# Rotating both token tiles on VectorE, and turning the attention rows by SBUF block moves instead of TensorE transposes

## The reference, cut to what matters

```
h = rmsnorm(x, g_mix);  z = h @ w_in            # 1024 x 5888
aq, ak, av, rq, rk, rv, rg, ga, gb = split(z)   # 512,128,128,512,512,1024,1024,1024,1024
aq, ak = rope_half(aq), rope_half(ak)           # 8 query heads, 2 key heads, of 64
ya = sliding_window_sink_attention(aq, ak, av, sinks) @ w_a
rq, rk = retention_rotation(rq), retention_rotation(rk)   # 4 heads of 128, pairs of neighbours
yb = (normed retention(rq, rk, rv) * silu(rg)) @ w_b
x = x + (sigmoid(ga) * ya + sigmoid(gb) * yb) @ w_out
x = x + square(relu(rmsnorm(x, g_mlp) @ w_up)) @ w_down
```

## Time and profile before

| what | value |
|---|---|
| median of the runs | 1015.03 us |
| profiled execution | 1015.36 us |
| its span | 1013.4 us |
| TensorE matmul busy | 1005.9 us, 99% |
| VectorE busy | 719.7 us, 71% |
| ScalarE busy | 504.4 us, 50% |
| GpSimd busy | 170.3 us, 17% |

### The profile page before, as it was taken

How to read it: one execution, slowest core, us unless ns; L and a number is a source line. 1 busy time by engine, 2 the same in 40 slices (tenths; PEclk the granted TensorE clock), 3 DMA queues, 4 the chain that set the end, 5 groups by cost and what they waited for, 6 DMA issues and landing times.

```text
span 1013.4 us, 13611 instructions
## 1 busy us (share of the span) xinstructions
PE 1005.9 (99%) x5677; PEld 851.7 (84%) x5677; DVE 719.7 (71%) x817; ACT 504.4 (50%) x620; POOL 170.3 (17%) x129
## 2 busy tenths in 40 slices
PE   9999999999999999999999999999999999999997
PEld 7888888888888888888788888888887899899796
DVE  5887746766565565797756667888877757789974
ACT  6545544454444545445554454444468545654352
POOL 0520010000000000430010020000000139159730
PEclk9999999999999999999999999999999999999999
DMA  9794455555555555594544557656654754355451
GB/s 337 252 306 128 163 166 166 169 175 196 193 184 206 166 176 178 186 293 164 166 150 142 168 147 279 197 185 208 199 175 135 233 182 166 125 166 145 116 188 42
DMA packets 100765, 185.47 MB, mean 183 GB/s; under 512 B 8840, under 2 KB 16096, under 8 KB 100576
## 3 DMA queue, kind: packets, MB, share of 16 engines
q1 hardware_dynamic: 100528, 184.51, 55.3%
q10 hardware_dynamic: 176, 0.09, 0.0%
HBM read 179.12 MB, written 3.15 MB: 180 GB/s over the span
## 4 chain that ended last, share of the span: by engine, by line
PE 99%; DMA 0%; DVE 0%; ACT 0%; SPq 0%; issue 0%; DVEq 0%; ACTq 0%
PE bank L766 14%; PE bank L768 12%; PE bank L769 12%; PE bank L1082 11%; PE bank L791 9%; PE bank L795 8%; PE bank L802 8%; PE bank L1086 6%; PE bank L1164 2%; PE bank L1388 1%; PE bank L964 1%; PE bank L948 1%; PE bank L773 1%; PE bank L783 1%; PE bank L1375 1%; PE bank L793 1%
## 5 line engine op out<-in xcount | busy, mean ns | idle before, releaser
L1868 DVE TENSOR_TENSOR w_lo<-arena,w_hi 128x2048 fp32r<-128x2048 f32 (+1 forms) x80 | 185.2, 2324 | 103.6 <-ACT w_hi L1476 103.3
L1868 DVE TENSOR_TENSOR w_lo<-raw,w_hi 128x2048 fp32r<-128x2048 f32 (+1 forms) x78 | 181.2, 2331 | 87.4 <-ACT w_hi L1476 87.2
L1476 ACT ACTIVATE w_hi<-raw 128x2048 fp32r<-128x2048 f32 (+1 forms) x83 | 157.1, 1893 | 100.3 <-PE bank L769 70.8
L1476 ACT ACTIVATE w_hi<-arena 128x2048 fp32r<-128x2048 f32 (+1 forms) x80 | 151.3, 1891 | 104.2 <-PE bank L769 80.4
L1082 PE MATMUL bank<-hT,w_hi 128*128 128x512 f32 x504 | 123.4, 391 | 0.0
L766 PE MATMUL bank<-w_hi,hT 128*128 128x512 f32 (+1 forms) x296 | 114.1, 386 | 0.0
L1082 PEld LDWEIGHTS bank<-hT,w_hi 128*128 128x128 f32 x504 | 92.2, 188 | 17.6
L2470 POOL TENSOR_TENSOR rstd<-mean,const 128x1 f32<-128x1 f32 (+1 forms) x16 | 9.1, 579 | 557.8 <-DVE mean L1877 388.5
L769 PE MATMUL bank<-w_hi,hT 128*128 128x512 f32 (+1 forms) x256 | 97.9, 382 | 0.0
L768 PE MATMUL bank<-w_lo,hT 128*128 128x512 f32 (+1 forms) x256 | 97.9, 382 | 0.0
L791 PE MATMUL bank<-w_hi,hT 128*128 128x512 f32 (+1 forms) x216 | 83.8, 391 | 0.0
(11 more groups left out here) (347 smaller groups left out, 1891.0 us busy)
## 6 DMA issues: line engine op xcount, KB each, us to landing
arena<-in_w_in SPq DMA_DIRECT2D x22, 1024.0 KB, 5.2
raw<-in_w_in SPq DMA_DIRECT2D x20, 1024.0 KB, 5.7
arena<-in_w_up SPq DMA_DIRECT2D x16, 1024.0 KB, 5.8
raw<-in_w_up SPq DMA_DIRECT2D x16, 1024.0 KB, 5.3
arena<-in_w_down SPq DMA_DIRECT2D x16, 1024.0 KB, 5.2
raw<-in_w_down SPq DMA_DIRECT2D x16, 1024.0 KB, 5.2
raw<-in_e_w_in SPq DMA_DIRECT2D x6, 1024.0 KB, 5.2
arena<-in_e_w_in SPq DMA_DIRECT2D x6, 1024.0 KB, 5.2
```

The source lines that it names most:

```text
L1476: act.activation(w_hi[:, p % SPLIT_RING, :, 0:n], raw_at(p)[:, :, 0:n], copy).then_inc(hi_ready, 1)
L1868: dve.tensor_tensor(w_lo[:, s, :, 0:n], raw_at(p)[:, :, 0:n], w_hi[:, s, :, 0:n].bitcast(F32), ALU.subtract).then_inc(lo_ready, 1)
```

## The change

`A_SLOTS` is 6: four pairs of query heads and two key heads. `rotate_halves` no longer writes the rotated queries in place and the keys to `ak_twice`; it writes all to `a_rows`, ordered by block of 32 features and then slot. Per layer, sixteen transfers of 48 KB from SBUF to SBUF (32 partitions, two rows of 768 bytes in each) move block b of token block i to partitions 32b to 32b + 31, and VectorE turns the result into `aT`, which is `aqT` and `akT` in one. SP issues them behind the four fetches of the retention rows, and ahead of the load of piece 14. VectorE turns them behind the retention rows and ahead of the split of piece 13. The twelve transposes, their three copies and GpSimd's rotations are gone. TensorE waits for `aT_ready` between the retention scores and the first attention scores.

```diff
-        ak_twice = area(16896, T, KV_HEADS * 2 * HEAD)
+        aT = area(11776, PAIRS + KV_HEADS, SEQ)
+        a_moved = area(15360, T * BLOCKS, A_SLOTS * BLOCK)
+        a_rows = area(16896, T, BLOCKS * A_SLOTS * BLOCK)
@@ rotate_halves
-            twice = ak_twice[:, t, :].rearrange("p (v c e d) -> p v c e d", v=KV_HEADS, c=2, e=2)
+            to = a_rows[:, t, :].rearrange("p (c e s d) -> p s c e d", c=2, e=2, s=A_SLOTS)
+            aq, bq = (v[:, 0:Q_HEADS, :, :].rearrange("p (i c) e d -> p i c e d", c=2) for v in (a4, b4))
             for e, op in ((0, ALU.subtract), (1, ALU.add)):
-                o.mark(eng.tensor_tensor(z[:, 0:Q_HEADS, e, :], a4[:, 0:Q_HEADS, e, :], b4[:, 0:Q_HEADS, e, :], op))
+                o.mark(eng.tensor_tensor(to[:, 0:PAIRS, :, e, :], aq[:, :, :, e, :], bq[:, :, :, e, :], op))
                 for c in range(2):
-                    last = eng.tensor_tensor(twice[:, :, c, e, :], a4[:, Q_HEADS:, e, :], b4[:, Q_HEADS:, e, :], op)
+                    last = eng.tensor_tensor(to[:, PAIRS:, c, e, :], a4[:, Q_HEADS:, e, :], b4[:, Q_HEADS:, e, :], op)
@@ SP, behind the load of piece 13
+                    fetch_blocks(r_moved, r_bounce, r_blocks)
+                    for t in range(T):
+                        sp.wait_ge(rope_done[t], l + 1)
+                    rows_out = a_moved.rearrange("p (t i) x -> p t i x", t=T)
+                    width = A_SLOTS * BLOCK
+                    for i in range(BLOCKS):
+                        for b in range(BLOCKS):
+                            sp.dma_start(rows_out[b * BLOCK:(b + 1) * BLOCK, :, i, :],
+                                         a_rows[i * BLOCK:(i + 1) * BLOCK, :, b * width:(b + 1) * width]).then_inc(a_blocks, 16)
@@ TensorE, window
-                if g == 4:
-                    (waits for both rotations, twelve transposes)
                 if g == 5:
                     pe.wait_ge(rT_ready, l + 1)
-                    pe.wait_ge(akT_ready, l + 1)
...
-                    pe.wait_ge(aqT_first, l + 1)
-                    pe.wait_ge(aqT_second, l + 1)
+                    pe.wait_ge(aT_ready, l + 1)
@@ VectorE
+            def turn_blocks(dst, src, slots, across=False):
+                rows_in = src.rearrange("p u (f s) -> p u s f" if across else "p u (s f) -> p u s f", s=slots)
+                return dve.transpose(dst.rearrange("p s (u q) -> p u s q", q=BLOCK), rows_in)
...
-                    rotate_pairs(dve, order, l, 0, z_ga, between=lambda part: step(l * PIECES + 2 * AQ + 1 + part))
+                    rotate_pairs(dve, order, l, 0, z_ga)
+                    step(l * PIECES + 2 * AQ + 1)
+                    rotate_pairs(dve, order, l, 1, z_gb)
+                    step(l * PIECES + 2 * AQ + 2)
                 if g == 3:
-                    rotate_halves(dve, order, l, 0, z_ga)
+                    for t in range(T):
+                        rotate_halves(dve, order, l, t, (z_ga, z_gb)[t])
...
                     if g == 5:
                         dve.wait_ge(r_blocks, 16 * BLOCKS * (l + 1))
-                        dve.transpose(rT.rearrange(...), r_moved.rearrange(...)).then_inc(rT_ready, 1)
+                        turn_blocks(rT, r_moved, 2 * RET_HEADS).then_inc(rT_ready, 1)
+                        dve.wait_ge(a_blocks, 16 * BLOCKS * BLOCKS * (l + 1))
+                        turn_blocks(aT, a_moved, A_SLOTS).then_inc(aT_ready, 1)
@@ GpSimd
-                rotate_pairs(pool, order, l, 1, z_gb)
-                rotate_halves(pool, order, l, 1, z_gb)
```

More of the change, by code:

```diff
@@ L34 @@
 BLOCKS = P // BLOCK
+A_SLOTS = PAIRS + KV_HEADS
 ATT2_HEADS = 4
@@ L400, in build_program @@
         rT_ready = sem("rT_ready")
[L401 to L404, removed]
+        a_blocks = sem("a_blocks")
+        aT_ready = sem("aT_ready")
         tanh_ready = sem("tanh_ready")
@@ L663, in load, with fetch_blocks @@
                 n[0] += 1
+            def fetch_blocks(dst, src, done):
+                for b in range(BLOCKS):
+                    at = slice(b * BLOCK, (b + 1) * BLOCK)
+                    sp.dma_start(dst[at, :, :], src.rearrange("(u q) (b x) -> b q u x", q=BLOCK, b=BLOCKS)[b]).then_inc(done, 16)
             def blocks_moved(l, piece):
@@ L987, in window @@
                     turn_vectors()
-                if g == 4:
-                    for t in range(T):
-                        pe.wait_ge(rope_done[t], l + 1)
+                if g == 5:
+                    pe.wait_ge(rT_ready, l + 1)
                     if l == 0:
                         pe.wait_ge(vec_ready, 3)
[L993 to L1000, removed]
-                    pe.wait_ge(akT_ready, l + 1)
                     for n in range(T):
@@ L1553, in window @@
                     vectors_turned()
[L1554 to L1558, removed]
                 if 6 <= g < 6 + PAIRS:
@@ L1980, in window @@
                     dve.wait_ge(vec_ready, 3)
-                    rotate_pairs(dve, order, l, 0, z_ga, between=lambda part: step(l * PIECES + 2 * AQ + 1 + part))
+                    rotate_pairs(dve, order, l, 0, z_ga)
+                    step(l * PIECES + 2 * AQ + 1)
+                    rotate_pairs(dve, order, l, 1, z_gb)
+                    step(l * PIECES + 2 * AQ + 2)
                 if g == 3:
-                    rotate_halves(dve, order, l, 0, z_ga)
-                if g == 4:
-                    dve.wait_ge(att_turned, 3 * l + 2)
-                    dve.tensor_copy(aqT[:, 2:4, :].rearrange("p i t -> p (i t)"), bank[:, 5, :]).then_inc(aqT_second, 1)
+                    for t in range(T):
+                        rotate_halves(dve, order, l, t, (z_ga, z_gb)[t])
                 if g == 5:
+                    dve.wait_ge(aT_ready, l + 1)
                     for n in range(T):
@@ L2114, in _ @@
                         dve.wait_ge(r_blocks, 16 * BLOCKS * (l + 1))
-                        dve.transpose(rT.rearrange("p s (u q) -> p u s q", q=BLOCK),
-                                      r_moved.rearrange("p u (s f) -> p u s f", f=BLOCK)).then_inc(rT_ready, 1)
+                        turn_blocks(rT, r_moved, 2 * RET_HEADS).then_inc(rT_ready, 1)
+                        dve.wait_ge(a_blocks, 16 * BLOCKS * BLOCKS * (l + 1))
+                        turn_blocks(aT, a_moved, A_SLOTS).then_inc(aT_ready, 1)
                     if g != AQ:
```

## The result

The changed kernel takes 1020.88 us (median of 4 runs, 1019.57 to 1023.02) against 1014.96 us for the kernel before, run beside it: a ratio of 1.0058, 95% interval 1.0045 to 1.0070. It is slower by 5.9 us where I forecast 2.6 us faster, and it lies above my range. Run again in a later group (label x11_after_again) it took 1020.3 us (median of 5), ratio 1.0048 (1.0036 to 1.0061).

What follows compares the result with a forecast made beforehand. TensorE, busy 99% of the span, was taken to bound the kernel. 1015.03 us minus 2.62 for the transposes plus 0 for new waits gave 1012.4 us; the 8-in-10 range was 1011.8 to 1016.8.

Steps and rivals of the forecast that it cites:

- The transposes' worth: TensorE, window 4: removing twelve transposes per layer saves 1.31 us each layer, 2.62 us in all.
- VectorE's rotation: VectorE rotating both tiles: 4.0 us for a tile's pairs, 3.5 for its halves, 15.0 per layer, hidden from TensorE.
- rival 1: SP's issues hold the loads back: at 0.71 us each, TensorE waits 1.9 us per layer before group 7, 1016.2 us; chance 0.32.
- rival 2: Blocks land late though issues are quick: turned rows 0.6 us late, 1013.6 us; chance 0.13.
- What it adds to SP: SP queue: fetches, sixteen issues, then load 14; free at 66.2, no wait for turned rows, load 14's lateness just covered.
- Start of the fetches: SP's four fetches of retention rows begin at 55.1, since the store goes out about 0.75 us earlier.
- Issue pace: SP's sixteen moves: 0.58 us per issue, the middle of two kinds of transfer, with ends at 0.46 and 0.91.
- Last landing: Last of the sixteen moves: issued at 65.6, lands 2.7 us later at 68.3; wanted at 69.8, so no wait.
- Bandwidth is not the limit: The moves carry 768 KB per layer in some 9 us, 83 GB/s, with no load in flight beside them.
- Load 14: Piece 14's load, behind the moves on SP: issued 66.2, landed 71.4, 0.9 us late, covered by 1.1 us to spare.
- Rival 1's formula: Wait per layer before group 7 from issue pace p: 56.9 + 16p + 5.2 - 70.47 - 1.1, a loss from p = 0.59.
- rival 3: VectorE's long instructions are its own, not waits on GpSimd: 12 us per layer, 1036 us; chance 0.03.

Runs made afterwards that it cites:

- experiment 2: Changed kernel with four moves of 192 KB over 128 partitions instead of sixteen, exchange of blocks left out (rows misplaced): 1013.31 us, ratio 0.9980 to the kernel before.
- experiment 1: Kernel before, with VectorE rotating both tiles and GpSimd none, TensorE still turning the attention rows: 1015.32 us against 1015.39, ratio 0.9999.
- experiment 7: Changed kernel with load 14 ahead of the moves, piece 13 split ahead of the turn, first attention scores behind group 6's first tile: 1014.68 us, ratio 0.9993.
- experiment 9: As experiment 7, with moves cut eight and eight around load 14, and load 13 held until the store has landed: 1020.16 us, ratio 1.0049.
- Experiment 6: Changed kernel with the sixteen moves contiguous, 1536 bytes per partition on either side, row order left wrong: 1021.46 us, one run.
- experiment 8: As experiment 7, with ScalarE fetching the retention rows and the moves issued eight ahead of load 14, eight behind: 1015.3 us, ratio 1.0001.
- second profile: Profile of the changed kernel, unaltered, from its run in a later group: median 1020.3 us.
- experiment 3: Changed kernel with the load of piece 14 ahead of the sixteen moves on SP: 1019.21 us, ratio 1.0040 to the kernel before.
- experiment 5: Changed kernel with VectorE's lower part of piece 13 ahead of the wait for the moves and the turn: 1021.43 us, ratio 1.0055 to the kernel before.

## Why the prediction was wrong

**Right.** The transposes' worth: experiment 2 shows it, 2.6 us over the two layers. VectorE's rotation: 1.22 and 0.68 us, about 3.7 us for the pairs of a tile and 3.0 for the halves, against 4.0 and 3.5; done at 55.6 against 56.4; free (experiment 1). The overlap with GpSimd as its cause fits too, a little less closely than I wrote: 1.22, 0.68 and 0.82 us alone are 0.12 to 0.14 us more than the 1.10, 0.56 and 0.68 us behind GpSimd's ends. The turn: 1.78 us against 1.76. The places where the loss could arise, and that the SP queue's pace decides: the waits stand where rivals 1 and 2 put them.

**Wrong: the step "What it adds to SP".** It said that SP is free of the sixteen at 66.2, that no wait arises for the turned rows, and that load 14 is just covered. The runs showed 68.74, waits of 2.0 and 0.5 us for the rows, and 2.3 us before group 7. In layer 0 all its terms erred to the same side:

- Start of the fetches: 56.49 against 55.1, +1.4 us. I let the store's earlier issue carry over to its landing. It left 0.4 us earlier and landed 0.8 us later than before, taking 8.5 us. It also took 8.4 to 8.9 us in experiments 1, 2, 7 and 9, with and without a load behind it. Its own data moved in 3.4 us before and in 3.5 us after (packets of 4096 bytes, 51.68 to 55.10 and 52.49 to 55.95). It starts when load 12's data are through: leaving earlier behind the same load gains nothing. And load 12 itself started more slowly: in its first two us it moved 166 packets of 2048 bytes, against 231 before; below, one window of the kernel before and of the changed one. In the kernel before the store was issued 1.2 us behind load 12 (47.14, 48.34), in the changed one 0.5 us behind (47.45, 47.94), as in all those of the experiments; whether that slows the load's start was not tested.

```profile
49.00:50.00 1.00, 1.00 (x6) 0.84 (x5) 1.00 (x1) 1.00 (x1) 1.00 (x1) 1.00 0.94 303
49.00:50.00 1.00, 1.00 (x6) 0.81 (x5) 1.00 (x2) 1.00 (x1) 0.00 (x0) 1.00 0.68 127
```

- Issue pace: 10.33 / 16 = 0.646 us against 0.58, +1.0 us over sixteen. I chose the middle of 0.46 and 0.71 because the moves have fewer rows. Experiment 6, one execution of it, shows the same pace with other rows; the nearest row of the same kind, SBUF to SBUF, should have stood, and 0.59 was my own bound for a loss. SP was free at 68.74 against 66.2 and my limit of 66.5.
- Last landing: 3.8 us against 2.7, +1.1 us. In layer 1, with load 14 as close behind, it was 2.0 us (454.75 to 456.71), so the load does not explain it; the cause is open. Together with a later start, the turn began at 71.98 where TensorE needed it to begin at 70.0: a wait of 2.0 us in layer 0, 0.5 in layer 1.
- "Bandwidth is not the limit": I counted the 768 KB of the moves and left out the 1 MB of retention rows fetched just ahead. Writing 32-partition blocks runs at about 200 GB/s (58 to 64 us), so those alone take 5 us. In the changed kernel that was over before it mattered: from 66 on the engines were a third busy, so there the pace of the issues held the last block back. When the issues came earlier (experiment 8) the engines took over. The Trainium skill (SBUF — State Buffer, "Door 1: The DMA port swizzle (why `[64,N]` ≈ `[32,N]`)") says that 32 adjacent partitions reach only half of the ports; 197 to 220 GB/s in experiment 8's windows against 373 and 375 agrees. The size of the rows is not the reason: in experiment 2 rows of the same 768 bytes, written to all 128 partitions, moved at 300 GB/s (last line; the first three are the changed kernel).

```profile
62.00:64.00 2.00, 2.00 (x11) 1.65 (x10) 2.00 (x1) 0.00 (x0) 0.00 (x0) 1.00 1.14 197
...
66.00:68.00 2.00, 2.00 (x10) 1.66 (x9) 2.00 (x1) 1.56 (x2) 0.00 (x0) 1.00 0.31 78
68.00:70.00 2.00, 2.00 (x12) 1.65 (x11) 0.02 (x1) 0.05 (x1) 0.00 (x0) 1.00 0.34 80
...
65.00:66.00 1.00, 1.00 (x6) 0.84 (x5) 0.00 (x0) 0.49 (x1) 0.00 (x0) 1.00 1.11 300
```

- Load 14: issued 68.79, ScalarE started at 74.55, against 66.2 and 71.4. Rival 1's formula, with the measured start and pace, 58.41 + 10.33 + 5.75 - 70.47 - 1.1, gives 2.9 us. In layer 1 the wait was 2.33 us. In layer 0 it was not seen, as TensorE itself had lost 3.6 us by then; in the second profile, where it had lost 1.1 us, it was 2.23 us. Experiments 3 and 5 show that this wait starts with load 14.

**Left out: the clock.** I priced a wait at its length. In layer 0 it cost 1.6 us more, through the slow stretch behind it. How much of that is net is not shown: TensorE, 1.6 us later, no longer waited for load 14's chain before group 7, as it did in layer 0 of the second profile (2.23 us), where no slow stretch came first. I had the two rivals as alternatives, too, and both came true. At the measured pace of 0.646 us rival 1's formula gives 0.84 us per layer, 1014.1 us; of my cases short of rival 3 only its dearest, 0.91 us per issue, lies past 1020 (1022.5), and no run had that pace. Rival 1, with a chance of 0.32, still named the right mechanism.

What stays open: why load 12 starts more slowly when the store follows it sooner, why the last block of layer 0 needs 3.8 us to land, and why the moves' issues cost 0.6 us where loads cost 0.4 to 0.5.

## What to carry to other kernels

Work taken from a full engine can come back as waits if it is replaced by many small transfers on a queue that loads also use: count issues times pace, and then ask when the first load behind them goes out. Price an issue by the nearest row of the same kind (source and destination memory), not by a mean with another kind; and count everything already in flight, at the rate of its own shape. A transfer issued sooner does not land sooner while an earlier one has the engines. Where the slack is 1 us and each of three terms may be off by 1 us, a loss deserves more than the 0.17 I gave it.

## What the runs showed of the hardware

A short wait of TensorE can cost more than its length. Over all profiles there are eleven waits in the layers of 1.69 us or more. With eight (1.69, 1.78, 1.99, 2.23, 2.38, 2.49, 2.83, 2.95 us) the granted clock fell to the lower level, for 3.4 us seven times and 6.8 us once, from 0.4 us before the wait's end (the longest) to 1.7 us behind it (in the changed kernel's layer 0 this cost 1.6 us); with three (1.90, 2.31, 2.33) it did not, and the same kernel had both: the changed kernel's profiles show it fall behind 1.99 and 2.23 us, and not behind 2.33 and 2.31. No shorter wait of the layers had a slow stretch behind it. This fits the spread of the changed kernel's runs, 1018.1 to 1023.0 us, where the kernel before stays within 1014.7 to 1016.1; that the spread comes from it was not tested.

The issue of a SBUF to SBUF move on SP takes 0.6 us (0.64 pace) over 32 partitions with either layout, and 0.67 to 0.70 us over 128 (experiment 2).
